# Gate branch of a two-block transformer: differential-attention rows turned ahead of the weight stream, linear-attention rows turned inside it

## What is computed

```python
o_hg = rms_norm(o_hg, hg_out_norm[l]) * jax.nn.silu(heads_hg(hog))
y_hg = o_hg.reshape(B, S, HG_WIDTH) @ w_branch_hg[l]
...
o_da = rms_norm(o_da, da_out_norm[l]) * (1.0 - lam_init)
y_da = o_da.reshape(B, S, DA_WIDTH) @ w_branch_da[l]
mixed = jax.nn.sigmoid(gate_hg) * y_hg + jax.nn.sigmoid(gate_da) * y_da
x = x + mixed @ w_out[l]
```

## Time and profile before

| | us |
|---|---|
| median of 3 runs | 2791.0 |
| lowest and highest run | 2788.99 and 2793.64 |
| the profiled execution | 2785.3 |
| its span | 2783.5 |
| branch stage begins (first DMA of SP) | 700.80 |
| first transpose of the stage | 701.60 |
| first matmul of the first weight tile | 718.61 |
| first matmul of the fifth weight tile | 729.5 |

### The profile page before, as it was taken

How to read it: one execution, slowest core, us unless ns; L and a number is a source line. 1 busy time by engine, 2 the same in 40 slices (tenths; PEclk the granted TensorE clock), 3 DMA queues, 4 the chain that set the end, 5 groups by cost and what they waited for, 6 DMA issues and landing times. The chain is left out here.

```text
span 2783.5 us, 37076 instructions
## 1 busy us (share of the span) xinstructions
PE 2658.3 (96%) x13640; PEld 2217.2 (80%) x13640; DVE 1848.3 (66%) x2538; ACT 1327.0 (48%) x1949; POOL 365.3 (13%) x311
## 2 busy tenths in 40 slices
PE   8999999998899899999999999889999999999999
PEld 7887776777788888888888888778888778888887
DVE  5770275457433688888888767656644874867978
ACT  3111143566432377778777421366643552535343
POOL 0222212100231122222222013000011000000000
PEclk9999999999999899999999999999999999999999
DMA  3114223410453399999999332000031625253441
GB/s 131 47 54 141 68 72 112 134 41 16 155 186 112 118 368 375 389 384 375 373 370 368 140 103 66 8 1 1 1 129 46 242 76 200 102 184 149 152 181 61
DMA packets 140823, 433.62 MB, mean 156 GB/s; under 512 B 23312, under 2 KB 45584, under 8 KB 108944
## 3 DMA queue, kind: packets, MB, share of 16 engines
q1 hardware_dynamic: 123584, 398.20, 39.6%
q0 software_dynamic: 10656, 20.99, 2.1%
q10 hardware_dynamic: 6448, 12.58, 1.3%
HBM read 385.58 MB, written 63.96 MB: 162 GB/s over the span
## 5 line engine op out<-in xcount | busy, mean ns | idle before, releaser
L2385 DVE TENSOR_TENSOR w_lo<-w_raw,w_hi 128x2048 fp32r<-128x2048 f32 x192 | 437.2, 2293 | 64.6 <-ACT w_hi L2319 60.3
L2319 ACT ACTIVATE w_hi<-w_raw 128x2048 fp32r<-128x2048 f32 x187 | 355.8, 1925 | 39.4 <-PE banks L2444 39.4
L3198 PE MATMUL banks<-b_parts,a_parts 128*128 128x512 f32 x1344 | 306.9, 390 | 6.3 <-DVE a_parts L3253 6.3
L3198 PE MATMUL banks<-a_parts,b_parts 128*128 128x512 f32 x1344 | 306.0, 389 | 2.3 <-DVE a_parts L3253 1.2
L3198 PEld LDWEIGHTS banks<-b_parts,a_parts 128*128 128x128 f32 x1344 | 251.8, 188 | 60.9 <-DVE a_parts L3253 8.8
L3198 PEld LDWEIGHTS banks<-a_parts,b_parts 128*128 128x128 f32 x1344 | 252.1, 188 | 55.1 <-DVE a_parts L3253 1.6
L634 POOL TENSOR_TENSOR w_lo<-w_raw,w_hi 128x512 fp32r<-128x512 f32 (+2 forms) x128 | 148.3, 1165 | 946.5 <-ACT w_hi L613 945.5
L3227 ACT ACTIVATE b_parts<-w_quarter 128x1024 fp32r<-128x1024 f32 x112 | 118.6, 1059 | 281.7 <-PE banks L3198 267.0
L613 ACT ACTIVATE w_hi<-w_raw 128x512 fp32r<-128x512 f32 (+2 forms) x128 | 70.8, 566 | 362.5 <-PE banks L686 341.7
L3247 DVE TENSOR_TENSOR b_parts<-w_quarter,b_parts 128x1024 fp32r<-128x1024 f32 x112 | 136.7, 1220 | 132.6 <-ACT b_parts L3227 132.5
L686 PE MATMUL banks<-w_hi,act_hi 128*128 128x512 f32 (+1 forms) x576 | 217.7, 378 | 6.9 <-DVE act_lo L1720 3.2
(11 more groups left out here) (515 smaller groups left out, 5583.7 us busy)
## 6 DMA issues: line engine op xcount, KB each, us to landing
w_raw<-in_w SPq DMA_DIRECT2D x192, 1024.0 KB, 7.6
a_parts<-scratch_x_parts SPq DMA_DIRECT2D x42, 1024.0 KB, 4.8
w_raw<-in_w_in SPq DMA_DIRECT2D x72, 256.0 KB, 2.7
w_quarter<-in_w_up SPq DMA_DIRECT2D x16, 1024.0 KB, 6.9
w_quarter<-in_w_down SPq DMA_DIRECT2D x16, 1024.0 KB, 7.3
scratch_x_parts<-a_parts SPq DMA_DIRECT2D x14, 1024.0 KB, 4.5
scratch_gateT<-gate_staged SPq DMA_DIRECT2D x32, 256.0 KB, 2.1
gate<-scratch_gateT SPq DMA_DIRECT2D x32, 256.0 KB, 3.2
```

The source lines that it names most:

```text
L2319: act.activation(hi[c % SLOTS][:, :], raw[c % TILES][:, :], ACT.Copy).then_inc(hi_done, 1)
L2385: dve.tensor_tensor(lo[c % SLOTS][:, :], raw[c % TILES][:, :], hi[c % SLOTS][:, :].bitcast(F32), ALU.subtract).then_inc(lo_done, 1)
L3198: mm = pe.matmul(out, left, right, start=(start and n == 0), stop=(stop and n == 2))
```

## The change

- The prelude of the branch stage is no longer `turn_rows` (which keeps its plain form for another stage) but a new class, `HalfPrelude`. It has sixteen pieces: n = 0 to 7 are the eight differential row tiles, n = 8 to 15 the eight linear ones.
- Pieces 0 to 7 are turned ahead of the first weight tile, into banks 0 to 7. TensorE then waits for `act_lo` of these eight alone.
- Pieces 8 to 15 are turned two at a time, after the weight tiles 0, 1, 2 and 3, into banks 4 to 7. After the last two TensorE waits for all sixteen `act_lo`. On ScalarE the two `act_hi` of such a pair stand in the queue after the gate step of tile i and ahead of `w_hi` of tile i + 1.
- The scaling of the differential rows is divided: VectorE scales row tiles 0 and 1, GpSimd row tiles 2 to 7, ahead of its first `w_lo`.
- In each column group the differential branch is now the first side (banks 0 to 3) and the linear one the second (banks 4 to 7); the gate blocks are loaded in the matching order.
- SP issues the first four weight tiles and their gate blocks ahead of the eight loads of the linear rows; before, the rows came first.

What each row means in the listings of the queues: line of the code, operation, output<-inputs by the names of the program, shape, count of equal rows in a run.

The core of the diff:

```diff
+class HalfPrelude:
+    HALF, EACH, OF_DVE = NT, 2, 2
...
+    def between(self, i):
+        return range(self.HALF + self.EACH * i, self.HALF + self.EACH * (i + 1)) if self.EACH * i < self.HALF else ()
...
+    def high(self, act, n):
+        act.wait_ge(self.turned, n + 1)
+        act.activation(self.part(self.v.act_hi, n), self.bank(n), ACT.Copy, scale=self.gain(n)).then_inc(self.hi_done, 1)
+    def scalar(self, act):
+        for n in range(self.HALF):
+            self.high(act, n)
+    def scalar_between(self, act, i):
+        for n in self.between(i):
+            self.high(act, n)
+    def gpsimd(self, pool):
+        for t in range(self.OF_DVE, NT):
+            self.scale(pool, t).then_inc(self.scaled, 1)
+    def vector(self, dve):
+        for t in range(self.OF_DVE):
+            self.scale(dve, t).then_inc(self.scaled_first, 1)
+        for n in range(2 * self.HALF):
+            dve.wait_ge(self.hi_done, n + 1)
...
+    def tensor(self, pe):
+        for n in range(self.HALF):
+            self.turn(pe, n)
+        pe.wait_ge(self.lo_done, self.HALF)
+    def tensor_between(self, pe, i):
+        for n in self.between(i):
+            self.turn(pe, n)
+        if self.between(i) and not self.between(i + 1):
+            pe.wait_ge(self.lo_done, 2 * self.HALF)
...
             for i, (tile, units, n) in enumerate(turns):
+                if split and 1 <= i <= RING:
+                    split.scalar_between(act, i - 1)
                 if i >= started:
                     high(act, i)
...
+                if split and i == RING - 1:
+                    split.sync(sp)
...
+                if split:
+                    split.tensor_between(pe, i)
...
-        tiles += group("tr", d["w_branch_hg"], HG_W // P, c0, c1, act, 0, 0)
-        tiles += group("tr", d["w_branch_da"], DA_W // P, c0, c1, act, HG_W // P, 4)
+        tiles += group("tr", d["w_branch_da"], DA_W // P, c0, c1, act, HG_W // P, 0)
+        tiles += group("tr", d["w_branch_hg"], HG_W // P, c0, c1, act, 0, 4)
```

More of the change, by code:

```diff
@@ L142, with __init__, part, bank_of @@
 class Prelude:
-    def __init__(self, sync, scalar, vector, tensor, ready):
-        self.sync, self.scalar, self.vector, self.tensor, self.ready = sync, scalar, vector, tensor, ready
+    def __init__(self, sync, scalar, gpsimd, vector, tensor, ready):
+        self.sync, self.scalar, self.gpsimd, self.vector, self.tensor, self.ready = sync, scalar, gpsimd, vector, tensor, ready
+class HalfPrelude:
+    HALF, EACH, OF_DVE = NT, 2, 2
+    def __init__(self, v, first, second, load, gains, scale):
+        sem = v.sem
+        self.v, self.load, self.gains, self.scale = v, load, gains, scale
+        self.pieces = [(t, x) for x in (first, second) for t in range(NT)]
+        self.turned, self.hi_done, self.lo_done = sem("turned"), sem("hi_done"), sem("lo_done")
+        self.scaled, self.scaled_first = sem("turn_scaled"), sem("turn_scaled_first")
+        self.rows_in = [sem(f"turn_rows_in{t}") for t in range(NT)]
+    def part(self, x, n):
+        t, (_, h) = self.pieces[n]
+        return x[:, 4 * h:4 * h + 4, t * P:(t + 1) * P]
+    def bank_of(self, n):
+        return self.v.bank[n % 8 if n < self.HALF else 4 + n % 4]
+    def bank(self, n):
+        return self.bank_of(n).rearrange("p (c t) -> p c t", c=4)
+    def gain(self, n):
+        h = self.pieces[n][1][1]
+        return self.gains[:, h:h + 1]
+    def between(self, i):
+        return range(self.HALF + self.EACH * i, self.HALF + self.EACH * (i + 1)) if self.EACH * i < self.HALF else ()
+    def sync(self, sp):
+        for t in range(NT):
+            self.load(sp, t).then_inc(self.rows_in[t], 16)
+    def high(self, act, n):
[15 more added lines that the diff above has]
+            dve.wait_ge(self.hi_done, n + 1)
+            dve.scalar_tensor_tensor(out=self.part(self.v.act_lo, n), in0=self.bank(n), scalar=self.gain(n), in1=self.part(self.v.act_hi, n).bitcast(F32),
+                                     op0=ALU.mult, op1=ALU.subtract).then_inc(self.lo_done, 1)
+    def turn(self, pe, n):
+        t, (rows_, _) = self.pieces[n]
+        if n >= self.HALF:
+            pe.wait_ge(self.lo_done, max(n - 3, self.HALF))
+            pe.wait_ge(self.rows_in[t], 16)
+        elif t < self.OF_DVE:
+            pe.wait_ge(self.scaled_first, t + 1)
+        else:
+            pe.wait_ge(self.scaled, t - self.OF_DVE + 1)
+        for c in range(4):
+            mm = pe.transpose(self.bank_of(n)[:, c * P:(c + 1) * P], rows_(t, c), self.v.ident[:, :])
+        mm.then_inc(self.turned, 1)
+    def tensor(self, pe):
[7 more added lines that the diff above has]
+            pe.wait_ge(self.lo_done, 2 * self.HALF)
@@ L1676, in _, with turn_rows @@
             weigh(n_units - 1)
-def turn_rows(v, chunk, order=None, load=None, gains=None, scale=None):
+def turn_rows(v, chunk):
     nc, sem = v.nc, v.sem
-    order = order or [(t, h) for t in range(NT) for h in range(2)]
+    order = [(t, h) for t in range(NT) for h in range(2)]
     turned, hi_done, lo_done = sem("turned"), sem("hi_done"), sem("lo_done")
-    rows_in = [sem(f"turn_rows_in{t}") for t in range(NT)] if load else None
-    scaled, link = sem("turn_scaled"), sem("turn_link")
     def part(x, n):
@@ L1699, in sync @@
     def sync(sp):
-        if load:
-            for t in range(NT):
-                load(sp, t).then_inc(rows_in[t], 16)
+        pass
     def scalar(act):
@@ L1706, in scalar, with gpsimd @@
             act.wait_ge(turned, n + 1)
-            g = {} if gains is None else {"scale": gains[:, order[n][1]:order[n][1] + 1]}
-            act.activation(part(v.act_hi, n), bank(n), ACT.Copy, **g).then_inc(hi_done, 1)
+            act.activation(part(v.act_hi, n), bank(n), ACT.Copy).then_inc(hi_done, 1)
+    def gpsimd(pool):
+        pass
     def vector(dve):
-        if scale:
-            for t in range(2):
-                scale(dve, t).then_inc(scaled, 1)
         for n in range(2 * NT):
-            if scale and n + 2 < NT:
-                scale(dve, n + 2).then_inc(scaled, 1)
             dve.wait_ge(hi_done, n + 1)
[L1718 to L1724, removed]
+            dve.tensor_tensor(part(v.act_lo, n), bank(n), part(v.act_hi, n).bitcast(F32), ALU.subtract).then_inc(lo_done, 1)
     def tensor(pe):
@@ L1774, in run @@
                 sp.wait_ge(free, n - 7)
-            sp.dma_start(gate[:, n % 8, :], d["gateT"][side, 2 * g + u % 2, :, u // 2 * N:u // 2 * N + N]).then_inc(gate_in[n % 8], 16)
+            sp.dma_start(gate[:, n % 8, :], d["gateT"][1 - side, 2 * g + u % 2, :, u // 2 * N:u // 2 * N + N]).then_inc(gate_in[n % 8], 16)
         return run
```

29 lines of the change are left out of this document (17 added, 12 removed).

## The result

| | before | changed |
|---|---|---|
| median of 14 runs, us | 2794.3 | 2802.57 |
| lowest and highest | 2781.98 and 2799.59 | 2795.38 and 2812.34 |
| profiled execution, us (span) | 2785.3 (2783.5) | 2801.42 (2799.4) |
| ratio of the runs, with its 95% interval | | 1.0033 (1.0023 to 1.0044) |

The changed kernel is slower by 0.33%, 9.2 us of 2794; the interval goes from 6.4 to 12.3 us. (The 2791.0 us shown ahead of the prediction was the median of the first three of these runs of before.) One run of experiment 6, of 4112 us, was in a slow state and is in none of the ratios.

What follows compares the result with a forecast made beforehand. TensorE, busy for 96% of the span, was taken to bound the kernel. -6.8 + 4.2 + 8.8 + 2.7 = +8.9 us on 2791.0 gave 2800 us, range 2794 to 2808.

Steps and rivals of the forecast that it cites:

- Start of tile 0, -6.8 us: Branch stage: with GpSimd scaling six row tiles at 1.295 us each, tile 0 starts at 711.8 instead of 718.6.
- the contention: Scaling ahead of tile 0: VectorE's two scalings could stand in GpSimd's way, adding at most their 1.36 us.
- the last scaling, on which the forecast was built: Ahead of tile 0: GpSimd's sixth scaling ends at 708.6, against 709.86 before; tile 0's start was reckoned from it.
- Transposes inside the stream, +4.2 us: Between tiles 0 to 3: TensorE turns four pairs of linear rows inside the stream, 1.04 us a pair.
- Pauses, +8.8 us: Ahead of tiles 1 to 4: TensorE waits 2.19 us behind each pair of turned linear rows, four times.
- The chain: Behind each pair: from the second act_hi through w_hi and w_lo to the next tile's first matmul, 1.91 us.
- Clock, +2.7 us at tile 0: Tile 0 runs wholly at 1.2 GHz, its twelve matmuls lasting 5.4 us; between 1.6 and 3.6 us lost.
- a sign of being wrong: Profile signs named as contradicting the forecast: pauses under 1 us, or a clock at full at tile 0.
- the turning ahead of tile 0 is the broken kind: Ahead of tile 0: 0.85 us of transposes in every 1.295 us of GpSimd, so the clock stays at 0.50.
- rival 1: Clock falls again at two of the three pauses ahead of tiles 2 to 4: +3.3 to +5.4 us; chance 0.17.
- Nothing for loads and sides: Linear rows loaded 3.6 us later still arrive in time, and exchanging the sides changes no instruction's size: no cost.
- The sum: Tile 4 starts, and the kernel ends, 8.9 us later; forecast median 2800 us, chance 0.48.

Runs made afterwards that it cites:

- experiment 6: Kernel before with the branch sides exchanged and the linear rows loaded after four weight tiles and gates, nothing else; ratio 1.0008 to the kernel before.
- experiment 8: experiment 1's kernel with linear rows turned 3, 3, 2 behind tiles 0 to 2, and GpSimd scaling only after VectorE's two; ratio 0.9976 to the kernel before, twice.
- experiment 1: Changed kernel with ScalarE preparing the next weight tile's high part and gate ahead of the pair of turned rows; ratio 0.9997 to the kernel before.
- experiment 4: Changed kernel with VectorE scaling all eight differential row tiles, alternating with act_lo, and GpSimd none; ratio 1.0061 to the kernel before.
- experiment 2: Changed kernel with linear rows turned four at a time behind tiles 0 and 1 instead of in pairs; ratio 1.0027 to the kernel before.
- experiment 3: Changed kernel with identity matmuls behind each pair of turned rows: 16 in its first kernel, ratio 1.0051 to the kernel before; then 8, ratio 1.0041.
- experiment 5: Kernel before with GpSimd scaling differential row tiles 2 to 7 and nothing else changed; ratio 0.9994 to the kernel before.

## Why the prediction was right, step by step

- *Start of tile 0, -6.8 us: -7.4.* GpSimd's six scalings took 6.93 us instead of 7.77: 1.04 us each, up to 1.49 us beside VectorE. The multiply with a broadcast operand was cheaper than the subtraction taken for it. The first transpose came 0.9 us later after the first DMA than before, since the two engines slowed each other; the prediction had noted the contention, but for GpSimd only. That late start bunched the row tiles: the last five `act_hi` ran back to back (3.15 us), and the last one began 0.5 us behind its transposes instead of 0.09. In experiment 8 GpSimd finished 0.5 us later and tile 0 still started 0.25 us earlier, so the last scaling, on which the forecast was built, didn't set the start alone.
- *Transposes inside the stream, +4.2 us: +4.1, four groups of 1.03 or 1.04 us.*
- *Pauses, +8.8 us: 3 x 2.03 + 2.13 = 8.2.* The chain was right link by link (second `act_hi`, `w_hi`, `w_lo`), and experiment 1 shows its cause.
- *Clock, +2.7 us at tile 0: wrong in its place.* Tile 0 ran at the upper level, which the prediction itself had named as a sign of being wrong. The turning had become denser (28 transposes in 4.87 us, where before 20 took 6.15 us), and the clock was back at 707.1. The step that failed is "the turning ahead of tile 0 is the broken kind": it set 0.85 us of transposing against 1.295 us of GpSimd, and GpSimd took 1.04. TensorE's late start closed the last gaps but wasn't needed, since in experiment 8 the clock came back as early without it. Instead the clock fell behind two of the pauses, 1.6 us each, +3.2. That is rival 1's mechanism, at the lower end of its price (3.3 to 5.4), behind the pauses ahead of tiles 1 and 3. In experiment 4, where VectorE paced the turning, tile 0 was slow as forecast, at 2.0 us instead of 2.7.
- *Nothing for loads and sides:* experiment 6.
- *The sum:* -7.4 + 4.1 + 8.2 + 3.2 = +8.1, and 0.4 us by which the four tiles are longer next to the transposes (2.85 against 2.75 us): +8.5, measured 8.6 in the stage, against 8.9 forecast. So close a hit is luck: two errors of the clock term cancelled, 2.7 too much at tile 0 and 3.2 missing later, and the falls are those of one execution. Without them the stage would have lost 5.4 us. The median of the changed kernel was 2802.6 us for 2800 forecast; that of the kernel before rose from 2791.0 to 2794.3 with more runs, so the two medians differ by 8.3 us.

## What to carry to other kernels

When work is moved in between the steps of a stream, write down for each engine what stands behind it in its queue: a step that waits for the new work holds everything after it, here the next weight tile, whose inputs were ready. Prepare the next step first and serve the inserted work second; the exchange of two statements was worth 10 us in the stage. Without it the move lost 8.6 us there, with it it won 1.8. And where VectorE and GpSimd would each read two SBUF operands at the same time, price both as slower; whether to keep them apart has to be timed (experiment 8: 0.2 us at tile 0).

## What the runs showed of the hardware

- GpSimd's in-place multiply of 128x512 float32 by a broadcast 4-column operand takes 1.04 us alone, its subtraction of two full operands 1.29 us.
- Two-operand work of VectorE and GpSimd at once costs both: VectorE's scaling goes from 0.69 to 1.55 us, GpSimd's from 1.04 to as much as 1.49 us.
- Of pauses of TensorE of about 2 us some were followed by a fall of its clock and some not, at the same place of the same code too. Of the ten unfilled pauses of 2.03 to 2.41 us between tiles (changed kernel, experiments 2 and 4) five were. Of the pauses ahead of tile 0, two of seven at 2.3 to 2.4 us were (the two are in experiment 2 and in the first kernel of experiment 3), both of experiment 8 at 1.98 us, and neither at 2.54 us (kernel before, experiment 6). What decides isn't shown. A fall cost 1.6 us in the changed kernel, and 1.4 to 1.6 us where it lay in tile 0 (experiments 2, 3, 5 and 8).
